# One product each for the convolution's mean and variance, and narrower level copies and products in an HGRN2 and mixture-of-experts layer

## The reference, cut to what matters

```
h  = depthwise_conv(glu(u)) + dw_b                    # 256 channels, 31 taps
mu = mean(h, channels)                                # convolution mean
var = mean((h - mu)**2, channels)                     # convolution variance
y_conv = silu((h - mu) * rsqrt(var + eps) * g + b)

# HGRN2, for each chunk of 64 tokens and each of 4 heads of width 64
b = cumsum(log_f)
A[t, s] = sum_d q[t,d] * k[s,d] * exp(b[t,d] - b[s,d])   for s <= t
o = (q * exp(b)) @ S + A @ v
```

## Time and profile before

| | us |
|---|---|
| median of 3 runs | 506.43 |
| lowest and highest run | 504.78, 508.18 |
| the profiled execution | 507.38 |
| its span, first to last instruction | 505.5 |
| TensorE busy in it | 479.1 |
| VectorE busy | 287.5 |
| ScalarE busy | 152.0 |

### The profile page before, as it was taken

The page is one execution under the profiler, slowest core; times in us unless marked ns, Lnnn a source line. Parts: engine busy times, 40 slices in busy tenths (PEclk is TensorE's granted clock), DMA queues, the critical chain, the costliest instruction groups (busy, mean ns, idle before and its releaser), DMA issues.

```text
span 505.5 us, 10941 instructions
## 1 busy us (share of the span) xinstructions
PE 479.1 (95%) x4474; PEld 321.3 (64%) x4474; DVE 287.5 (57%) x703; ACT 152.0 (30%) x373; POOL 39.4 (8%) x47
## 2 busy tenths in 40 slices
PE   7999999999999999999999997999999999985695
PEld 6888899888795444565656654575565555553452
DVE  3898999999687875327474332332353222232256
ACT  2440238530246333330243221222222211111134
POOL 0100000000000000000111030302102111000000
PEclk9999999999999999999999998999999999989799
DMA  8991000000009999339789999799999999999994
GB/s 271 350 373 79 0 1 1 1 1 1 3 3 334 384 427 411 162 148 362 288 280 358 423 358 397 288 407 428 420 422 422 428 418 426 422 425 426 416 379 175
DMA packets 29378, 143.02 MB, mean 283 GB/s; under 512 B 4645, under 2 KB 11973, under 8 KB 20624
## 3 DMA queue, kind: packets, MB, share of 16 engines
q1 hardware_dynamic: 23360, 131.03, 65.3%
q0 software_dynamic: 5536, 10.85, 6.2%
q10 hardware_dynamic: 432, 0.44, 0.3%
HBM read 133.73 MB, written 17.30 MB: 299 GB/s over the span
## 4 chain that ended last, share of the span: by engine, by line
PE 84%; DMA 8%; DVE 4%; issue 1%; ACT 1%; DVEq 0%; SPq 0%; POOLq 0%
PE bank_pair L1853 15%; PE bank_pair L1532 15%; PE bank_pair L1730 11%; PE bank_pair L1876 8%; PE bank_pair L1861 6%; PE bank_pair L1542 4%; DMA area_g<-expert_out 3%; PE bank_pair L1482 3%; PE bank_pair L1846 3%; PE bank_pair L1884 3%; PE bank_pair L1668 3%; DMA expert_out<-area_m,cols 2%; DMA expert_out<-area_m,cst 2%; PE bank_pair L1497 1%; PE bank_pair L1746 1%
## 5 line engine op out<-in xcount | busy, mean ns | idle before, releaser
L1730 PE MATMUL bank_pair<-area_w,area_m 128*128 128x512 f32 x128 | 56.7, 594 | 0.6 <-issue 0.6
L911 DVE SCALAR_TENSOR_TENSOR area_m<-area_g,cols,area_m 128x512 f32<-128x512 f32 x60 | 41.3, 743 | 0.0
L1730 PEld LDWEIGHTS bank_pair<-area_w,area_m 128*128 128x128 f32 x128 | 23.6, 190 | 27.1 <-issue 27.1
L1853 PE MATMUL bank_pair<-area_w,area_m 128*64 128x256 f32 x320 | 38.7, 384 | 0.4 <-issue 0.4
L1853 PEld LDWEIGHTS bank_pair<-area_w,area_m 128*64 128x64 f32 x320 | 22.4, 136 | 14.7 <-issue 4.0
L1853 PE MATMUL bank_pair<-area_g,area_m 128*64 128x256 f32 x256 | 31.1, 385 | 0.0
L2080 DVE COPY cst<-bank_pair 128x128 f32<-128x128 f32 (+1 forms) x38 | 9.9, 261 | 31.8 <-PE bank_pair L1867 23.0
L2098 DVE COPY area_m<-bank_pair 64x512 f32<-64x512 f32 x20 | 13.9, 694 | 24.6 <-PE bank_pair L1876 24.6
L1861 PE MATMUL bank_pair<-area_w,area_m 128*32 128x128 f32 x576 | 21.8, 302 | 3.8 <-DMA area_w<-in_w_exp 3.8
L2087 DVE TENSOR_TENSOR cst<-cst,bank_pair 128x128 f32<-128x128 f32 x22 | 6.4, 289 | 32.7 <-ACT cst L2001 32.7
L1853 PEld LDWEIGHTS bank_pair<-area_g,area_m 128*64 128x64 f32 x256 | 17.1, 136 | 11.7 <-issue 3.1
(11 more groups left out here) (425 smaller groups left out, 876.3 us busy)
## 6 DMA issues: line engine op xcount, KB each, us to landing
area_g<-in_w_exp SPq DMA_DIRECT2D x14, 2048.0 KB, 25.8
area_w<-in_w_exp SPq DMA_DIRECT2D x13, 2048.0 KB, 17.7
area_w<-in_w_exp SPq DMA_DIRECT2D x16, 1024.0 KB, 15.7
area_g<-in_w_exp SPq DMA_DIRECT2D x14, 1024.0 KB, 27.7
area_x<-in_w_exp SPq DMA_DIRECT2D x4, 2048.0 KB, 19.5
area_w<-in_w_in SPq DMA_DIRECT2D x6, 1024.0 KB, 14.0
area_w<-in_w_out SPq DMA_DIRECT2D x2, 2048.0 KB, 14.8
expert_out<-area_g SPq DMA_DIRECT2D x2, 2048.0 KB, 23.8
```

The lines of the kernel that those rows point to most:

```text
L911: ins = V.scalar_tensor_tensor(out=mixT[:, i, :], in0=src, scalar=w, in1=mixT[:, i, :], op0=ALU.mult, op1=ALU.add)
L1730: ins = T.matmul(bank[7][:, :], mixT[:, k, j * P:(j + 1) * P], w_out_sb[:, n, k, :], start=(k == 0), stop=(k == KT - 1))
L1853: ins = T.matmul(out_b[h * BC:(h + 1) * BC, 0:2 * P], x[:, k, :], w_gate_up[slot][:, :, k, h * P:(h + 1) * P], start=(k == 0), stop=(k == ...
```

## The change

Four edits, on VectorE and TensorE:

1. VectorE adds the two convolution tiles into `osq[:, 0]`, between the last tap and the addition S15, and `conv_sums` is one product of that sum.
2. ScalarE's squares stay as they are. VectorE adds the two squared tiles into `osq[:, 0]` behind taking 3, waiting for ScalarE's squares, and `conv_squares` is one product of that sum.
3. The predicated copies of the six levels take only the query halves: 256 of 512 columns, in runs of h.
4. At level 0 the products are of the 32 keys by the 32 queries that meet, so 32 stationary and 32 moving columns over the same 64 rows, in place of 64 and 64.

```diff
@@ -1037,6 +1037,8 @@
             conv(5)
             add_part("q1", U2)
             conv(TAPS - tap[0])
+            dve.wait_ge(conv_done, 2)
+            V.tensor_tensor(osq[:, 0, :], mixT[:, 0, :], mixT[:, 1, :], ALU.add).then_inc(conv_done, 1)
             add_part("q1", S15)
 
             dve.wait_ge(u_done, 1)
@@ -1104,23 +1106,29 @@
             for n in range(2 * (nl + 1)):
                 ti, l = n % 2, (nl - n // 2)
                 dve.wait_ge(g_done, n + 1)
-                m = cst[:, K_MASK + l * CHUNK:K_MASK + (l + 1) * CHUNK].unsqueeze(1).to_broadcast([P, NC_, CHUNK])
-                g = bank[2 + n % 2][:, :].rearrange("p (c t) -> p c t", t=CHUNK)
-                a = A[:, ti, :].rearrange("p (c t) -> p c t", t=CHUNK)
+                m = cst[:, K_MASK + l * CHUNK:K_MASK + (l + 1) * CHUNK]
                 if n >= 2:
                     dve.wait_ge(g_used, n - 1)
                 if l == nl:
-                    V.tensor_tensor(a, g, m, ALU.mult).then_inc(g_used, 1)
+                    g, a = (v.rearrange("p (c t) -> p c t", t=CHUNK) for v in (bank[2 + n % 2][:, :], A[:, ti, :]))
+                    V.tensor_tensor(a, g, m.unsqueeze(1).to_broadcast([P, NC_, CHUNK]), ALU.mult).then_inc(g_used, 1)
                 else:
-                    V.copy_predicated(a, m.bitcast(I32), g).then_inc(g_used, 1)
+                    h = LEVELS[l]
+                    pairs = CHUNK // (2 * h)
+                    g, a = (v.rearrange("p (c r t) -> p c r t", c=NC_, r=pairs)[:, :, :, h:] for v in (bank[2 + n % 2][:, :], A[:, ti, :]))
+                    m = m.bitcast(I32).rearrange("p (r t) -> p r t", r=pairs)[:, :, h:].unsqueeze(1).to_broadcast([P, NC_, pairs, h])
+                    V.copy_predicated(a, m, g).then_inc(g_used, 1)
                 if n == MEANS_AT:
                     dve.wait_ge(conv_means, 1)
                     for i in range(2):
                         V.tensor_tensor(mixT[:, i, :], mixT[:, i, :], bank[7][:, :], ALU.subtract).then_inc(cen_done, 1)
+                if n == SQUARES_AT - 1:
+                    dve.wait_ge(conv_factor, 1)
+                    V.tensor_tensor(osq[:, 0, :], osq[:, 0, :], osq[:, 1, :], ALU.add).then_inc(conv_factor, 1)
                 if n in ADD_AT:
                     add_part("q1", C12 + ADD_AT.index(n))
                 if n == NORM_AT:
-                    dve.wait_ge(conv_factor, 2)
+                    dve.wait_ge(conv_factor, 3)
                     for i in range(2):
                         V.tensor_tensor(mixT[:, i, :], mixT[:, i, :], ed[0][:, 0, :], ALU.mult).then_inc(cnorm, 1)
                 if n == SCORES_AT + 1:
@@ -1605,17 +1613,13 @@
             mean = cst[:, K_MEAN:K_MEAN + P]
 
             def conv_sums():
-                pe.wait_ge(conv_done, 2)
+                pe.wait_ge(conv_done, 3)
                 pe.wait_ge(d_rest, 16)
-                for i in range(2):
-                    ins = T.matmul(bank[7][:, :], mean, mixT[:, i, :], start=(i == 0), stop=(i == 1))
-                ins.then_inc(conv_means, 1)
+                T.matmul(bank[7][:, :], mean, osq[:, 0, :], start=True, stop=True).then_inc(conv_means, 1)
 
             def conv_squares():
-                pe.wait_ge(conv_factor, 1)
-                for i in range(2):
-                    ins = T.matmul(bank[7][:, :], mean, osq[:, i, :], start=(i == 0), stop=(i == 1))
-                ins.then_inc(conv_means, 1)
+                pe.wait_ge(conv_factor, 2)
+                T.matmul(bank[7][:, :], mean, osq[:, 0, :], start=True, stop=True).then_inc(conv_means, 1)
 
             def scores(u):
                 p, g, i = u // 2, u % 2, u % 2
@@ -1635,7 +1639,7 @@
             def hgrn_output(ti):
 
                 if ti == 0:
-                    pe.wait_ge(conv_factor, 2)
+                    pe.wait_ge(conv_factor, 3)
                     pe.wait_ge(g_used, 2 * nl + 1)
                 else:
                     pe.wait_ge(orstd, ti)
@@ -1663,6 +1667,11 @@
                         t = slice(c * CHUNK, (c + 1) * CHUNK)
                         if l == nl:
                             kk, qq = kf[s, ti, META + c * CHUNK:META + (c + 1) * CHUNK], qf[s, ti, t]
+                        elif l == 0:
+
+                            h = CHUNK // 2
+                            kk, qq = lev[0][s, ti, c * CHUNK:c * CHUNK + h], lev[0][s, ti, c * CHUNK + h:(c + 1) * CHUNK]
+                            s, t = slice(s.start, s.start + h), slice(c * CHUNK + h, (c + 1) * CHUNK)
                         else:
                             kk = qq = lev[l][s, ti, t]
                         ins = T.matmul(bank[2 + n % 2][s, t], kk, qq, start=True, stop=True)
```

## The result

The changed kernel takes 503.25 us (median of 20 runs, 500.8 to 504.98) against 506.77 us (20 runs, 503.44 to 508.5) for the kernel before in the same comparison: ratio 0.9943, 95% interval 0.9923 to 0.9963. The profiled execution took 501.65 us, its span 499.7.

A forecast was written before the change was run, and what follows sets the result against it. The prediction took TensorE to bound the kernel, with VectorE nearly level; 1.15 us from single products plus 0.1 from narrow ones made 1.25 us, so 506.43 - 1.25 = 505.2 us, range 502.8 to 507.8.

The forecast's parts named there:

- the case of no gain: Rival behind the mixer: the gain ends in a wait for weights or the last scatter and gather; 506.4 us, chance 0.15.
- all its mechanisms: Whole kernel: bounds over the forecast's mechanisms, gains from 0.7 to 1.9 us, up to halved products with a quicker copy.
- What bounds the kernel: Whole span: TensorE, busy for 95%, sets the time; VectorE is nearly level in the loop, so savings need it to keep up.
- Part 1: Sums and squares on TensorE: one product costs 1.05 us against 1.91 for two, saving 1.72 us together at most.
- Part 2: Addition ahead of S15 on VectorE: takes 0.68 us and holds up the projection's part P3 by 0.3 us (0.2 to 0.4).
- Part 3: From sums to squares: half copies take 0.46 us, TensorE waits for the second addition, group 5 gains 1.15 of 1.72 us.
- The rival built on it: Predicated copies in short runs cost up to 1.45 us each, slowing the kernel to 511 us; chance 0.04.
- Part 4: Groups 5 to 11: TensorE sets the pace, the 1.15 us gain passes unchanged, shorter copies are worth nothing of their own.
- Part 5: The 32 by 32 products: 29 ns for a record, saving 0.1 to 0.15 us for both groups, bounds -0.1 to 1.0.
- Part 6: End of the loop: TensorE sets the start of `hgrn_output(0)`, 1.25 us earlier, and no new wait holds scores(1).
- The narrow products take half the time: Rival at level 0: group 13 ends at 146.5, group 12's copy holds `hgrn_output(0)` to 147.05; gain 1.65 us, chance 0.12.
- The price for changing the tile shape: Rival at level 0: going into and out of the new shape costs 0.2 us; gain 1.05 us, 505.4 us, chance 0.12.

The follow-up runs named there:

- the kernel before again: The kernel before, unedited, timed and profiled once more against itself: 506.09 us, ratio 1.0004 (0.9970 to 1.0037).
- the loop's gain taken back: The changed kernel plus two idle products of 512 columns ahead of `hgrn_output(0)`, against the kernel before: 505.34 us, ratio 1.0014 (0.9979 to 1.0050).
- that of the second: The changed kernel, unedited, timed again against the kernel before: 503.10 us, ratio 0.9973 (0.9936 to 1.0010).

## Why the prediction was right, and where it was wrong

It said 505.2 us, within 1%, and the range holds the 503.25 measured. That says little for the mechanism: the range of 502.8 to 507.8 is mostly the spread of single runs, and holds the case of no gain too (by its own terms its upper end is 506.4 + 1.7 = 508.1). The medians differ by 3.5 us where 1.25 were forecast, so that the median came out inside is in part luck. Stage B is the measure of the sum: 1.75 us there, above the 0.7 to 1.5 of the forecast and inside the 0.7 to 1.9 of all its mechanisms. By its steps:

- **What bounds the kernel** holds. Held back by 1.89 us ahead of `hgrn_output(0)`, the kernel loses 1.89 us in B; no later wait takes it in.
- **Part 1** holds: one product with its start is 1.06 us (sums) and 1.12 (squares).
- **Part 2** holds, its price slightly above the forecast: the addition takes 0.69 us, and P3 is held up by 0.38 against 0.3 (0.2 to 0.4), group 0 behind it by 0.48. The run with this addition on GpSimd got 0.49 back.
- **Part 3** holds in its result. The squares' product starts at 133.42 and group 5 at 134.55 on the chain. Stage A ended 1.30 us earlier in this profile than in the one the prediction was read from; with that added, they are 134.72 against 134.7 and 135.85 against 135.75. But its way there was partly another. "I count nothing for its short runs" is wrong: up to runs of 2 the copy takes 0.73 us, not 0.46. L1003 reads SBUF without a mask, and was no measure for a predicated copy out of PSUM. It cost 0.1 us, since the second addition waited for VectorE to be through with the copy of group 3 (it starts 0.53 to 0.54 us after this copy in every run with half copies and this addition) in place of the squares, done at 132.51. It was one of the prediction's own signs of a wrong forecast (over 0.6 us at level 5). The rival built on it needed 0.95 us.
- **Part 4** is wrong where it calls the shorter copies worth nothing and lets TensorE set the pace. From the start of group 11 to `hgrn_output(0)` it takes 3.11 us with whole copies, and 2.85 with half ones and wide products. That is 0.26 us, since before the change groups 12 and 13 and `hgrn_output(0)` started 0.15 us behind the end of a copy. Half copies alone give 0.34 in B.
- **Part 5 is the step that failed.** Not 29 ns but 16 for a record inside a group, about half: the prediction's own sign of a wrong forecast (20 ns or less) came true. The two groups save 0.76 us, of which 0.41 arrive at `hgrn_output(0)` in place of the 0.1 to 0.15 forecast. Of the 0.35 between, 0.10 are the price of the changed shape and 0.25 are spent ahead of group 13 and of `hgrn_output(0)`, where VectorE's copies set the start; at the latter, which is 0.11 of them, the change of shape back would have cost nearly as much anyway. The row the forecast rested on was misread: L1795 has 3 moving columns but 64 stationary ones, and the runs with one narrow side show that the wider side sets the time. The bound of -0.1 to 1.0 us held it. The Trainium skill, TensorEngine Tiling, section Performance Considerations, has a product with a free dimension of 1 cost as much as one of 60; for products of two 64-row halves the runs show 16 ns for 32 by 32 against 29 for 64 by 64, so that rule agrees with them only while the other side stays at 64.
- **Part 6** is wrong on who sets the start of `hgrn_output(0)`: it is VectorE's copy of group 12, not TensorE, by a margin of 0.01 to 0.02 us over the pause of 0.15 that the change of shape takes with narrow keys. That no new wait stands behind it holds: `scores(1)` starts at 147.65 (A + 130.99; before A + 132.76).

**The rivals.** What happened is closest to the one that had 0.12, "The narrow products take half the time": its copy of group 12 holds `hgrn_output(0)` to 147.05, and with the 1.30 us of stage A added it started at 146.94, a gain of 1.77 us where that rival has 1.65. The price for changing the tile shape, the other rival with 0.12, is there as well, 0.10 us in and 0.10 out, as it says, but beside products of half the time.

So 1.08 us at group 5, 0.02 more up to group 11, 0.26 from the copies in groups 11 to 13, and 0.41 from the narrow products make 1.77 at `hgrn_output(0)`, where 1.74 and 1.77 are seen against the kernel before again, and 1.75 in B. Alone the three parts give 1.02, 0.34 and 0.10, 1.46 in sum: the narrow products pay only where the copies are short as well.

**What stays open.** 1.75 us of 506.8 make a ratio of 0.9965, a little above the interval of the first comparison and inside that of the second. No profile shows a second place at which the change gives something, and with the loop's gain taken back the ratio is 1.0014. Whether the first comparison owes its further 1.1 us to the spread of A, C and E among runs, the runs don't tell; the 4.4 us between the shortest and the longest A would be enough for it. Nor do they show why half the runs have a slow A.

## What to carry to other kernels

Where two engines are nearly level, cost an edit with its partner: narrow products were worth 0.10 us behind whole copies and 0.36 behind half ones. To see who sets a start there, compare it with the end of the work that it waits for; the chain of waits, which goes by modelled ends on TensorE, showed no VectorE where VectorE decided. And take the spacing of small records inside a group, not from a mean that has a pause in it. Read from a row only what its shape shows, both operands of a product, and for a copy its source, mask and run. And compare stages that start at the same instruction; here spans differed by 5.8 us where the change made 1.75.

## What the hardware showed that was not expected

- Float32 matmul records over 64 rows, by turns in the two halves of the rows, start in pairs inside a group: two every 58 ns with 64 by 64 columns, 45 with 48 by 48 (group 11 with all levels narrow), 32 with 32 by 32, and 56 or 58 with one side alone at 32.
- A change of the loaded columns from 64 to 32 or back costs 0.10 us (a pause of 0.15 in place of 0.05 us); a change of the moved columns alone costs nothing.
- A group of level products, or `hgrn_output(0)`, starts 0.15 us behind the end of the copy that it waits for.
- A predicated copy of 256 columns out of PSUM takes 0.43 us in runs of 4 or more elements, and 0.73, as a whole one of 512, in runs of 1 or 2.
- TensorE's granted clock fell to 0.61 at 232 to 236 us while it was busy for 4.00 of 4.00 us; it followed the router's products of 36 columns (L1746, 32 records from 227.8 us on) and cost 1.7 us. 3 of 14 profiles have it; the other 11 ran the same products without it.
- The products behind the first load of the input ran at 0.44 or 0.22 us each with no edit there, and A ended between 16.6 and 21.1 us.
